# Two blocks of the last conditioning product moved from the router's stage into the wait of the linear attention, and one expert load held back for a gather

## The chip, the cores and the metric

The kernel runs on one core of one Trainium2 chip. The metric is the device time of one execution in microseconds (us). Three timed runs of the kernel before gave a median of 1047.66 us (1046.27 to 1048.70).

## The reference

Two layers of a diffusion backbone over 256 latent tokens `x` and 256 context tokens `ctx`, width 1024, all float32. Cut to what the change touches:

```python
for l in range(DEPTH):                                   # DEPTH = 2
    mod = (silu_c @ ada_w[l] + ada_b[l])                 # shift, scale, gate twice: 6 x 1024
    cmod = silu_cc @ ada_w[l] + ada_b[l]
    h_lat, h_ctx = modulate(x, sh1, sc1), modulate(ctx, csh1, csc1)
    if l % 2 == 0:                                       # layer 0
        o_ctx, s_f, s_b = even_mixer(h_ctx, 0, 0, ...)   # linear attention | convolution, one output projection
        o_lat, _, _ = even_mixer(h_lat, s_f, s_b, ...)
    else:                                                # layer 1: attention
        o_lat, o_ctx = odd_mixer(...)
    x = x + g1 * o_lat
    y = hier_moe(tokens, ...)                            # top-1 group of 4, top-2 experts of 4 in it
    x = x + g2 * y
return rms_norm(x) * final_norm_g

# gla_chunked, per head (4 heads), chunks of 64 tokens, in both directions:
att = where(mask, q_t @ k_t.T, 0)                        # scores inside a chunk
u   = k_end.T @ v                                        # what a chunk adds to the state
s   = decay * s + u                                      # recurrence over the chunks
o   = att @ v + q_t @ s_prev                             # inside + across
```

## The kernel before

Everything is written out by hand for the five engines, which meet only at semaphores. TensorE (PE) runs, in this order: the input projections of layer 0, `gla`, `even_out`, `rows_and_router(0)`, `experts(0)`, the attention of layer 1, its output projection, `rows_and_router(1)` and `experts(1)`. Products write one of eight PSUM banks `ps[:, b, :]` of 512 columns.

**Weights** go through a ring of six slots of 2 MB (`ring`, three more blocks have places of their own in `xh` and `gm`). `weight_stream` lists the blocks in the order in which PE uses them, and `ring_places` gives each block the slot of the block that is freed six before it. SyncE (SP) issues the loads in that order (`load`, L515; in the expert loop L563) and waits before each until PE has freed its slot, so a load can't be issued before the block six places ahead of it has been used. Behind the input projections the list was `eout` 0 and 1 (the two halves of the output projection), `ada` 8 to 11 of layer 1, then the experts: `g`, `u`, `d` for gate, up and down of one expert. `moe_stream` issues for layer 0: g0, u0, g1, u1, d0, g2, then u2, whose place in `xh` is free once the router's rows have been read (`h2_ps`), then d1 and so on.

**Conditioning.** `ada_block(g, n)` (L627) multiplies the two conditioning vectors by a 2 MB block of `ada_w`, 16 matmuls of 512 columns. Group 4 is the last third of layer 1's: its four blocks all add into bank 5 (`ADA_BANK[4]`). VectorE's (DVE) `ada_added(4)` (L1829) adds that bank to the bias row once all four are done, and PE waits for this before the first expert's down product. Two of the blocks ran in the router's first wait (while DVE chose the experts, `chosen`), two behind the index products of the first two experts.

**Linear attention** (`gla`) treats the four heads as two pairs `pt`. For each pair PE turns the decayed keys (`turn_keys`, L847), makes the scores, which DVE masks and adds (`masked`, L2398 and L2406) into SBUF, makes the chunk sums u for the directions d = 0, 1 (`chunk_sums`), the part inside the chunks (`inside`, L874), and, once DVE's `recurrence` (L2418, L2421) has written 14 states, the part `across` (L888). ScalarE (ACT) copies the turned keys (`keys_taken`, L1641), copies and squares the outputs (`outputs_taken`, L1648), and takes roots (`output_roots`, L1657) of what `square_sums` adds up on PE. `KV_BANK` names the banks of the chunk sums, `O_BANK` those of the outputs. The sum of squares of a head was written over its own output's bank. `even_out` (L948) starts with the convolution's channels (c = 4 to 7) and comes to the attention's channels when DVE has normed them (`normed_outputs`).

**Router and first gather.** In `rows_and_router(0)` PE turns the normed rows back (L975), ACT stores them to `h2_rows` in DRAM, DVE picks the experts and the row numbers. GpSimd (POOL) then gathers the first expert's 96 rows from DRAM (L2654, semaphore `xg_in0`), PE makes the slot product (L614, `ps<-ar` 128x32, waits `slots_ready`), turns the gathered rows (`first_xt`, L1136) and starts the experts' gate and up products (L614 and L1054).

## Time and profile before

| | us |
|---|---|
| median of three timed runs | 1047.66 |
| the profiled execution, its own time | 1039.51 |
| its span in the trace | 1037.7 |
| PE busy | 949.4 (91% of the span) |
| DVE busy | 623.6 (60%) |
| ACT busy | 178.0 (17%) |
| POOL busy | 114.9 (11%) |
| moved by DMA | 311.94 MB, mean 301 GB/s |

Busy shares are means over stages with different limits. Linear attention lies at 219 to 256 us of the span, the output projection at 256 to 316, the router at 316 to 352, the experts of layer 0 at 352 to 616, the attention of layer 1 to about 790, the experts of layer 1 from about 812. "PEclk" is the clock that TensorE was granted, in parts of 2.4 GHz: 0.50 is 1.2 GHz. A float32 matmul counts as two records. "Idle before <-releaser" is the time an engine stood before an instruction, and what ended it.

### The profile page before, as it was taken

Reading aid. Unit: us, or ns where it says so; the run is one execution under the profiler, and the core shown is the slowest. Engines: PE = TensorE matmul, PEld = TensorE weight load, DVE = VectorE, ACT = ScalarE, POOL = GpSimd, SP = SyncE. Lnnn points to the kernel's source line nnn. Section 1 sums busy time; section 2 is a strip of 40 time slices with the busy share of each in tenths; the row PEclk is TensorE's granted clock in tenths of the full one; section 3 lists DMA queues with packets and bytes.
Section 4 is the critical chain, followed back from the end, with each engine's and each line's share of the span. In section 5 each row is a group of like instructions: output and inputs, shape, how many; then the busy total and the mean of one; then the engine's idle time right before and its main releaser. Section 6 shows DMA issues by size and latency. Waiting matters only on the chain.

```text
span 1037.7 us, 19786 instructions
## 1 busy us (share of the span) xinstructions
PE 949.4 (91%) x7940; PEld 575.5 (55%) x7940; DVE 623.6 (60%) x1516; ACT 178.0 (17%) x339; POOL 114.9 (11%) x176
## 2 busy tenths in 40 slices
PE   3999999989998799999999997997997999988896
PEld 1443433457445588988988973443646455543442
DVE  1200799787456586676675636467435977775553
ACT  2100022353024010000000013225413000000001
POOL 7100100102300100000001132100101100000000
PEclk9999999997999699999999998999997999999999
DMA  9999876442826999999999959646034989999994
GB/s 332 398 392 369 327 268 218 164 163 84 250 91 243 383 357 362 403 417 405 391 402 407 424 181 356 245 167 237 6 104 180 346 339 400 399 385 412 417 429 171
DMA packets 51354, 311.94 MB, mean 301 GB/s; under 512 B 7096, under 2 KB 8888, under 8 KB 33632
## 3 DMA queue, kind: packets, MB, share of 16 engines
q1 hardware_dynamic: 36752, 277.88, 68.2%
q0 software_dynamic: 9376, 21.19, 6.7%
q10 hardware_dynamic: 5168, 12.06, 3.1%
q8 instruction: 41, 0.67, 0.3%
q14 instruction: 17, 0.14, 0.0%
HBM read 300.52 MB, written 17.25 MB: 306 GB/s over the span
## 4 chain that ended last, share of the span: by engine, by line
PE 69%; DMA 16%; DVE 9%; issue 2%; SPq 2%; ACT 2%; POOL 0%; ACTq 0%; DVEq 0%; POOLq 0%
PE ps L614 46%; PE ps L1054 9%; DMA ring<-in_moe_w_gate 8%; PE ps L948 3%; PE ps L627 3%; DMA ring<-in_moe_w_down 2%; DMA ring<-in_ada_w 2%; PE ps L1097 2%; PE ps L1175 2%; SPq L515 2%; DMA y_rows<-ar 1%; PE ps L888 1%; DMA xh<-y_rows,sm 1%; DMA ar<-h_rows,sm 1%; PE ps L1418 1%
## 5 line engine op out<-in xcount | busy, mean ns | idle before, releaser
L614 PE MATMUL ps<-ring,ar 128*32 128x384 f32 (+6 forms) x3872 | 479.8, 466 | 17.9 <-DMA ring<-in_moe_w_gate 13.7
L614 PEld LDWEIGHTS ps<-ring,ar 128*32 128x32 f32 (+2 forms) x3872 | 198.7, 121 | 145.3 <-issue 87.1
L1054 PE MATMUL ps<-ring,ar 128*32 128x128 f32 x1488 | 167.8, 275 | 0.0
L1054 PEld LDWEIGHTS ps<-ring,ar 128*32 128x32 f32 x1488 | 163.7, 111 | 2.7
L2171 DVE STREAM_TRANSPOSE ar<-ar 32x256 f32<-32x256 f32 x304 | 132.2, 435 | 5.0 <-issue 0.6
L614 PE MATMUL ps<-xh,ring 128*128 128x512 f32 x256 | 114.9, 603 | 0.7 <-DMA ring<-in_even_w_in 0.7
L2214 DVE TENSOR_TENSOR ar<-ar,ps 128x384 f32<-128x384 f32 (+2 forms) x33 | 15.9, 482 | 132.1 <-PE ps L1054 68.1
L614 PE MATMUL ps<-ring,xh 128*128 128x512 f32 x192 | 85.9, 604 | 1.9 <-ACT xh L1478 1.6
L614 PEld LDWEIGHTS ps<-xh,ring 128*128 128x128 f32 x256 | 48.3, 192 | 64.2 <-issue 62.9
L2343 DVE SCALAR_TENSOR_TENSOR ar<-ar,cpar 128x512 f32<-128x512 f32 x120 | 79.6, 742 | 0.0
L1530 ACT ACTIVATE ar<-ps 128x384 f32<-128x384 f32 (+2 forms) x33 | 14.3, 433 | 289.7 <-PE ps L614 205.7
L614 PEld LDWEIGHTS ps<-ring,xh 128*128 128x128 f32 x192 | 36.5, 193 | 48.6 <-issue 45.6
L2201 DVE STREAM_TRANSPOSE ar<-ar 32x64 f32<-32x64 f32 x256 | 60.5, 236 | 4.5
L2193 DVE STREAM_TRANSPOSE ar<-ar 32x128 f32<-32x128 f32 x144 | 59.5, 413 | 2.9
L1097 PE MATMUL ps<-ring,ar 128*32 128x256 f32 x256 | 57.9, 379 | 0.0
L2650 POOL COPY sm<-sm 96x1 int32 (+3 forms) x32 | 6.0, 187 | 342.4 <-DVE ar L2171 318.3
L627 PE MATMUL ps<-ring,silu_c 128*32 128x512 f32 x320 | 39.9, 619 | 0.0
L2311 DVE TENSOR_TENSOR ar<-ps,gm 128x512 f32<-128x512 f32 x12 | 8.3, 689 | 51.7 <-PE ps L614 39.8
L1097 PEld LDWEIGHTS ps<-ring,ar 128*32 128x32 f32 x256 | 28.0, 110 | 18.1
L614 PE MATMUL ps<-ar 128*128 128x512 f32 (+3 forms) x112 | 33.3, 464 | 4.6 <-ACT ar L1767 2.4
L1535 ACT ACTIVATE ar<-ps 128x512 f32<-128x512 f32 x16 | 9.6, 598 | 149.3 <-PE ps L614 149.3
L2654 POOL DMA_INDIRECT ar<-h_rows,sm x32 | 31.2, 976 | 27.9 <-POOL sm L2650 26.8
(371 smaller groups left out, 908.9 us busy)
## 6 DMA issues: line engine op xcount, KB each, us to landing
ring<-in_moe_w_gate SPq DMA_DIRECT2D x31, 2048.0 KB, 17.1
ring<-in_moe_w_up SPq DMA_DIRECT2D x30, 2048.0 KB, 15.6
ring<-in_moe_w_down SPq DMA_DIRECT2D x30, 2048.0 KB, 19.1
ring<-in_ada_w SPq DMA_DIRECT2D x24, 2048.0 KB, 10.5
ring<-in_even_w_in SPq DMA_DIRECT2D x5, 2048.0 KB, 14.0
y_rows<-ar POOLq DMA_DIRECT2D x17, 384.0 KB, 10.5
ring<-in_odd_w_in SPq DMA_DIRECT2D x3, 2048.0 KB, 18.1
y_rows<-ar ACTq DMA_DIRECT2D x16, 288.0 KB, 8.9
```

The source lines that it names most:

```text
L515: sp.dma_start(wide, s).then_inc(arrival(i), 16)
L614: return nc.tensor.matmul(o, l, r, start=start, stop=stop)
L627: m = nc.tensor.matmul(ps[32 * q:32 * q + 32, ADA_BANK[g], :], silu_c[:, 2 * k + c, 10 - 2 * s:42 - 2 * s], w[:, c, 512 * q:512 * q + 512] ...
L948: m = nc.tensor.matmul(ps[:, j, :], mix[:, c, j * P:(j + 1) * P], blk(i)[:, c, :], start=(c == 4), stop=(c == 3), skip_group_check=True)
L1054: m = nc.tensor.matmul(ps[96:128, bank, g * P:(g + 1) * P], xgT[:, p, c, 32 * g:32 * g + 32], w[:, c, 3 * P:HID], start=c == 0 and g == 0, ...
L1097: nc.tensor.matmul(ps[96:128, 5, 256 * g:256 * g + 256], tokens(g, c), w[:, c, 768:D], start=c == 0 and g == 0, stop=c == HC - 1 and g == ...
L1175: m = nc.tensor.matmul(acc(j, h), mixw[64 * h:64 * h + 64, p, j * P:(j + 1) * P], yb[64 * h:64 * h + 64, p, 0:512], start=False, stop=True ...
L2171: m = V.transpose(xgT[32 * q:32 * q + 32, p, :, slots], xg[slots, p, :].rearrange("s (c q i) -> s q c i", c=KC, q=4)[:, q, :, :])
L2193: V.transpose(hidT[32 * q:32 * q + 32, p, :, 32 * r:32 * r + 32], cols[:, q, :, :])
L2201: m = V.transpose(hidT[32 * q:32 * q + 32, p, 0:2, 32 * r:32 * r + 32], cols[:, q, :, :])
L2343: V.scalar_tensor_tensor(acc[n], u_in[:, n, :, bass.ds(t, 256)], cpar[:, n, bass.ds(t, 1)], acc[n], ALU.mult, ALU.add).then_inc(sem("conv_ ...
L2654: G.indirect_dma_start(xg[0:CAP[l], p, :], None, h2_rows, bass.IndirectOffsetOnAxis(ap=idxc[0:CAP[l], p:p + 1], axis=0), bounds_check=NT * ...
```

## The change

1. Blocks 8 and 9 of layer 1's `ada` stand in the stream ahead of `eout`. PE runs them (group 4, n = 0 and 1) in `gla` ahead of `across(0)`, into bank 6; DVE adds them between `decayed(1)` and `masked(1)`, and `scores(1)` waits for that, since it writes bank 6.
2. Blocks 10 and 11 (n = 2, 3) take the place of 8 and 9 in the router's first wait, into bank 5. Nothing stands any more behind the index products. DVE's `late_added` stands where `ada_added(4)` stood.
3. `chunk_sums(0, 1)` is cut in two: the even chunks (bank 1) go ahead of `inside(0, 0)`, the odd ones stay. `chunk_sums(1, 1)` writes banks 0 and 2 in place of 5 and 7 and moves ahead of `inside(1, 0)`, behind a wait for the first two outputs' copies.
4. The sums of squares have banks of their own (`SQ_BANK`); those of heads 0 and 1 move behind `inside(1, 1)`, and `even_out` no longer waits for the first two roots. ACT takes the second pair's keys before the first pair's outputs.
5. SP waits for the first gather's landing before it issues u2 of layer 0.

```diff
-    tail = [("eout", 0, 0), ("eout", 0, 1)] + ada(1, 8, 9, 10, 11) + moe_blocks(0)
+    tail = ada(1, 8, 9) + [("eout", 0, 0), ("eout", 0, 1)] + ada(1, 10, 11) + moe_blocks(0)
...
-        KV_BANK = (((4, 5), (1, 3)), ((1, 3), (5, 7)))
+        KV_BANK, SQ_BANK = (((4, 5), (1, 3)), ((1, 3), (0, 2))), ((5, 7), (4, 6))
...
-        ADA_BANK = (6, 2, 3, 2, 5)
+        ADA_BANK = (6, 2, 3, 2, 6)
+        LATE_BANK = 5
...
                     sp.wait_ge(sem("h2_ps"), NT)
+                    sp.wait_ge(sem("xg_in0"), 16)
                     expert_load("u", 2)
...
-                            m = nc.tensor.matmul(ps[32 * q:32 * q + 32, ADA_BANK[g], :],
+                            m = nc.tensor.matmul(ps[32 * q:32 * q + 32, LATE_BANK if g == 4 and n >= 2 else ADA_BANK[g], :],
...
-                chunk_sums(0, 0)
+                chunk_sums(0, 0).then_inc(sem("kv_sum"), 1)
                 pe.wait_ge(sem("att_masked"), 2)
+                chunk_sums(0, 1, range(0, NCH, 2))
                 inside(0, 0)
                 pe.wait_ge(sem("att_masked"), 4)
-                chunk_sums(0, 1)
+                chunk_sums(0, 1, range(1, NCH, 2)).then_inc(sem("kv_sum"), 1)
                 inside(0, 1)
                 pe.wait_ge(sem("qk_exp"), 8)
                 pe.wait_ge(sem("ke_diff"), 4)
+                ada_block(4, 0)
+                ada_block(4, 1)
                 across(0)
                 turn_keys(1)
+                pe.wait_ge(sem("ada_added"), 6)
                 scores(1)
-                square_sums((0, 1))
                 pe.wait_ge(sem("ketok_ready"), 4)
-                chunk_sums(1, 0)
+                chunk_sums(1, 0).then_inc(sem("kv_sum"), 1)
+                pe.wait_ge(sem("o_taken"), 2)
+                chunk_sums(1, 1).then_inc(sem("kv_sum"), 1)
                 pe.wait_ge(sem("att_masked"), 6)
                 inside(1, 0)
                 pe.wait_ge(sem("att_masked"), 8)
-                chunk_sums(1, 1)
                 inside(1, 1)
+                square_sums((0, 1))
                 across(1)
...
                 pe.wait_ge(sem("conv_ready"), NPT)
-                pe.wait_ge(sem("o_root"), 2)
...
                 if l == 0:
                     pe.wait_ge(sem("h2_act"), 2)
-                    ada_block(4, 0)
-                    ada_block(4, 1)
+                    ada_block(4, 2)
+                    ada_block(4, 3)
...
-                    pe.wait_ge(sem("h2_act"), NT)
-                    ada_block(4, 2)
-                    ada_block(4, 3)
...
+                keys_taken(1)
                 outputs_taken(0)
-                keys_taken(1)
...
                 decayed(1)
+                ada_added(4)
                 masked(1)
```

PE's program from the turned keys of the second pair to the end of linear attention; `ar,xh 64x128` are chunk sums, L874 (now L877) is `inside`, `ar,cst 128x512` the sums of squares, L888 (now L891) `across`. Before:

```order
L614 MATMUL ps<-xh 128x128 x15
L614 MATMUL ps<-ar,cst 128x512 [waits o_taken] x2
L614 MATMUL ps<-ar,xh 64x128 [waits ketok_ready]
L614 MATMUL ps<-ar,xh 64x128 x15
L874 MATMUL ps<-xh,ar 128x128 [waits att_masked]
L874 MATMUL ps<-xh,ar 128x128 x3
L614 MATMUL ps<-ar,xh 64x128 [waits att_masked]
L614 MATMUL ps<-ar,xh 64x128 x15
L874 MATMUL ps<-xh,ar 128x128 x4
L888 MATMUL ps<-xh,ar 128x64 [waits state]
```

The same place in the changed kernel:

```order
L616 MATMUL ps<-xh 128x128 x15
L616 MATMUL ps<-ar,xh 64x128 [waits ketok_ready]
L616 MATMUL ps<-ar,xh 64x128 x15
L616 MATMUL ps<-ar,xh 64x128 [waits o_taken]
L616 MATMUL ps<-ar,xh 64x128 x15
L877 MATMUL ps<-xh,ar 128x128 [waits att_masked]
L877 MATMUL ps<-xh,ar 128x128 x3
L877 MATMUL ps<-xh,ar 128x128 [waits att_masked]
L877 MATMUL ps<-xh,ar 128x128 x3
L616 MATMUL ps<-ar,cst 128x512 [waits o_taken] x2
L891 MATMUL ps<-xh,ar 128x64 [waits state]
```

Both directions' chunk sums now stand ahead of the first wait for the masks, and the sums of squares behind both `inside`. SP's loads around the router in the changed kernel (`ring` is a ring slot, `xh` the place of u2):

```order
L516 DMA ring<-in_moe_w_down 128x4096 [waits block_used]
L516 DMA ring<-in_moe_w_gate 128x4096 [waits block_used]
L516 DMA xh<-in_moe_w_up 128x4096 [waits xg_in0,h2_ps]
L516 DMA ring<-in_moe_w_down 128x4096 [waits block_used]
L516 DMA ring<-in_moe_w_gate 128x4096 [waits block_used]
```

These are d0, g2, u2, d1 and g3. The order of the expert loads is the old one; what each waits for has moved: g0 and u0 now wait for `ada` 8 and 9, g1 and u1 for `eout` 0 and 1, d0 and g2 for `ada` 10 and 11.

## Rows read from the trace of the kernel before

**Rows 1.** Page, the chain that ended last, shares by engine
```profile
PE 69%; DMA 16%; DVE 9%; issue 2%; SPq 2%; ACT 2%; POOL 0%; ACTq 0%; DVEq 0%; POOLq 0%
```

**Rows 2.** Timeline, PE, linear attention: start, us, what, [idle before <-releaser]
```profile
219.36 1.04 PE L847 MATMUL ps<-cst,gm 128*128 128x128 f32 x8
220.32 2.06 PE L614 MATMUL ps<-gm 64*128 64x128 f32 x32
...
227.09 1.16 PE L874 MATMUL ps<-gm,ar 128*128 128x128 f32 x8
230.84 6.03 PE L888 MATMUL ps<-gm,ar 64*128 64x64 f32 x56 [2.59 <-DVE ar L2421]
236.80 1.97 PE L847 MATMUL ps<-cst,xh 128*128 128x128 f32 x8
238.69 3.30 PE L614 MATMUL ps<-xh 64*128 64x128 f32 x32
...
250.57 5.36 PE L888 MATMUL ps<-xh,ar 64*128 64x64 f32 x56 [2.42 <-DVE ar L2421]
255.86 4.95 PE L948 MATMUL ps<-ring,ar 128*128 128x512 f32 x8
...
262.36 24.20 PE L948 MATMUL ps<-ring,ar 128*128 128x512 f32 x56
```

**Rows 3.** Windows: stretch, length, busy PE PEld DVE ACT POOL, PEclk, DMA share, GB/s
```profile
228.00:231.00 3.00, 0.41 (x6) 0.25 (x5) 3.00 (x12) 2.99 (x4) 0.00 (x0) 1.00 0.00 0
231.00:233.00 2.00, 2.00 (x23) 2.00 (x23) 2.00 (x4) 2.00 (x4) 0.00 (x0) 0.52 0.00 0
...
253.00:256.00 3.00, 3.00 (x29) 2.88 (x27) 2.93 (x4) 0.05 (x1) 0.00 (x0) 0.50 0.00 0
```

**Rows 4.** Timeline, DVE, linear attention
```profile
227.51 3.17 DVE L2421 SCALAR_TENSOR_TENSOR ar<-ar,ps 128x128 f32<-128x128 f32 x12
...
238.09 0.48 DVE L2390 MEMSET xh<- 128x512 f32 x1 [3.79 <-PE ps L847]
...
247.13 0.29 DVE L2418 COPY ar<-ps 128x128 f32<-128x128 f32 x1 [1.33 <-PE ps L614]
```

**Rows 5.** Timeline, ACT, the second pair's keys
```profile
239.29 1.08 ACT L1641 ACTIVATE xh<-ps 128x512 f32<-128x512 f32 x2
```

**Rows 6.** Timeline, SP, the four `ada` loads and g0
```profile
180.98 38.94 SPq L515 DMA_DIRECT2D ring<-in_ada_w  x4
286.59 0.34 SPq L515 DMA_DIRECT2D ring<-in_moe_w_gate  x1
```

**Rows 7.** Timeline, PE, router to the first expert
```profile
327.70 3.64 PE L627 MATMUL ps<-ring,silu_c 128*32 128x512 f32 x32
...
341.63 1.97 PE L614 MATMUL ps<-ar 128*128 128x32 f32 x16 [0.57 <-DVE ar L2060]
349.66 1.51 PE L1136 MATMUL ps<-cst,ar 96*128 96x96 f32 x8 [6.06 <-DMA ar<-h_rows,sm]
351.96 0.86 PE L614 MATMUL ps<-ring,ar 128*32 128x384 f32 x3 [0.78 <-DVE ar L2165]
```

**Rows 8.** Gathers of `h2_rows`: first of layer 0, four in its experts, first of layer 1
```profile
L2654 POOL DMA_INDIRECT ar<-h_rows,sm x1: 1025/1025/1025, 339.1 to 339.1; - x1
DMA to landing us min/median/max: 10.4/10.4/10.4
...
DMA to landing us min/median/max: 9.5/10.2/10.8
...
DMA to landing us min/median/max: 3.0/3.0/3.0
```

**Rows 9.** Windows, first experts, columns as in rows 3
```profile
356.00:364.00 8.00, 8.00 (x141) 7.80 (x133) 6.20 (x16) 0.49 (x1) 0.51 (x2) 0.91 1.01 367
```

**Rows 10.** Expert loads issued 400 to 530 us, and PE's waits at 480 to 600
```profile
DMA to landing us min/median/max: 9.7/18.2/28.6
...
PE ps L614 <- DMA ring<-in_moe_w_gate: 2.0, 2, 1.9
```

More of the change, by code:

```diff
@@ L463, in ada_last @@
             l, a, n = ADA_GROUPS[g]
-            return at["ada", l, 2 + h if g == 0 else 2 * (a + n) - 1]
+            return at["ada", l, 2 + h if g == 0 else 9 if g == 4 else 2 * (a + n) - 1]
         def xn_of(k):
@@ L626, in ada_block @@
                         for q in range(4):
-                            m = nc.tensor.matmul(ps[32 * q:32 * q + 32, ADA_BANK[g], :],
+                            m = nc.tensor.matmul(ps[32 * q:32 * q + 32, LATE_BANK if g == 4 and n >= 2 else ADA_BANK[g], :],
                                                  silu_c[:, 2 * k + c, 10 - 2 * s:42 - 2 * s], w[:, c, 512 * q:512 * q + 512],
-                                                 start=n == 0 and c == 0, stop=True, skip_group_check=True)
+                                                 start=n == (2 if g == 4 and n >= 2 else 0) and c == 0, stop=True,
+                                                 skip_group_check=True)
                     m.then_inc(sem("block_used"), 1)
@@ L837, in square_sums @@
                     pe.wait_ge(sem("o_taken"), h + 1)
-                    mm(ps[:, O_BANK[h // 2][h % 2], :], ones, (qT if h % 2 == 0 else kT)[:, h // 2, :])\
+                    mm(ps[:, SQ_BANK[h // 2][h % 2], :], ones, (qT if h % 2 == 0 else kT)[:, h // 2, :])\
                         .then_inc(sem("o_sumsq"), 1)
@@ L860, in scores, with chunk_sums @@
                         m.then_inc(sem("att"), 1)
-                def chunk_sums(pt, d):
-                    for n in range(NCH):
+                def chunk_sums(pt, d, chunks=range(NCH)):
+                    for n in chunks:
                         lo = CHUNK * (n % 2)
@@ L869, in chunk_sums @@
                                    v_tok[lo:lo + 64, n // 2, (2 * pt + hh) * P:(2 * pt + hh + 1) * P])
-                    m.then_inc(sem("kv_sum"), 1)
+                    return m
                 def inside(pt, hh):
@@ L1159, in down @@
                 if l == 0 and isinstance(e, int) and e == 0:
-                    pe.wait_ge(sem("ada_added"), 6)
+                    pe.wait_ge(sem("ada_added"), 7)
                 if not (isinstance(e, int) and e == 0) and not narrow(l, e):
@@ L1656, in output_roots @@
                     act.wait_ge(sem("o_sumsq"), 2 * pt + hh + 1)
-                    A_((qT if hh == 0 else kT)[:, pt, :], ps[:, O_BANK[pt][hh], :], ACT.Sqrt, scale=1.0 / DV, bias=eps)\
+                    A_((qT if hh == 0 else kT)[:, pt, :], ps[:, SQ_BANK[pt][hh], :], ACT.Sqrt, scale=1.0 / DV, bias=eps)\
                         .then_inc(sem("o_root"), 1)
@@ L1830, in ada_added, with late_added @@
                                            ALU.add, ALU.add).then_inc(sem("ada_added"), 1)
+            def late_added():
+                dve.wait_ge(sem("block_used"), at["ada", 1, 11] + 1)
+                V.tensor_tensor(modrow_of(4), modrow_of(4), ps[:, LATE_BANK, :], ALU.add).then_inc(sem("ada_added"), 1)
             def mean_square(n, width, count):
@@ L2243, in experts @@
                     rows_placed()
-                    ada_added(4)
+                    late_added()
                 if l == 1:
@@ L2596, in mod_rows @@
                 l, a, n = ADA_GROUPS[g]
-                pool.wait_ge(sem("ada_added"), g + 2)
+                pool.wait_ge(sem("ada_added"), 7 if g == 4 else g + 2)
                 for s in range(n // 2):
```

## The prediction, made before the changed kernel was run

> **What bounds the kernel now.** I read the chain that ended last first. It is 69% PE, 16% DMA and 9% DVE [rows 1], so PE's own order decides most of the time, and what can be gained lies in the places where PE stands or is slow. Next, PE's timeline with its idle times. Linear attention has two: 2.59 us before `across(0)` and 2.42 us before `across(1)`, both ended by DVE's recurrence [rows 2]. The windows beside them show what follows: PE was busy for 0.41 of the 3 us before 231, and from 231 on the granted clock was 0.52, that is 1.2 GHz; the second idle ends in 0.50 at 253 to 256 [rows 3]. So `turn_keys(1)` took 1.97 us where the same eight records had taken 1.04, and `scores(1)` 3.30 where they had taken 2.06 [rows 2]. In the router PE stood 6.06 us for the first expert's gather, which took 10.4 us from issue to landing [rows 7, 8], and ran the first experts at the low clock. After that PE has work without a break until late in the loop, where it waits 1.9 us for a gate load [rows 10]. What is won before 352 us therefore moves the whole rest, unless the loads don't follow.
>
> **Linear attention.** (a) The even half of `chunk_sums(0, 1)`, 0.55 us, goes into PE's wait for the second mask, so `inside(0, 1)`, which ended at 228.25 (227.09 + 1.16), ends at about 227.7. The two blocks cost what two cost in the router, 3.64 us at the full clock [rows 7], and end at 231.35. The states were there for 230.84 [rows 2]: `across(0)` starts at 231.4, **0.6 us late**. (b) PE now has no gap of any size between 220 and 231, and I take the clock to stay full. `across(0)` isn't in the trace at full clock; the eight turned keys give a ratio of 1.97 to 1.04, so 6.03 becomes 3.2. That is 2.8, with 0.9 for the keys and 1.2 for the scores **4.9 us**. `scores(1)` ended at 242.0 and now ends at 237.7. (c) From there DVE leads: masks, sums, recurrence. In it DVE stood 1.33 us for `chunk_sums(1, 1)`, which waited for the last mask itself [rows 4]. It now runs ahead of `inside(1, 0)`: **1.3 us**. Its new wait is for ACT: two copies of keys in 1.08 us [rows 5], then four copies and squares of a bank, which I put at the same length or a little more each, begun half a microsecond behind `across(0)` at 235.2 and done at about 238.9, while PE reaches the wait at 238.8. Behind it stand `inside(1, 0)` and `inside(1, 1)` and the sums of squares, two matmuls of 512 columns each like those of the projection (0.43 a record, 24.20 / 56 [rows 2]), some 5 us in all but for the wait for the last mask, done by about 244.6, and the recurrence, 3.6 us behind the last mask at 241.2, ends at 244.8. So `across(1)` starts at 244.9 where it started at 250.57, with almost no idle before it. (d) Then it too runs at the full clock, 3.2 for 5.36: **2.1 us**. The first eight records of `even_out` took 4.95 where 56 took 24.20, so 3.5 at full clock: **1.4 us**. The sum is 4.9 - 0.6 + 1.3 + 2.1 + 1.4 = **9.1 us** by the first sums of `even_out`.
>
> What I cost at nothing here: DVE's added `ada_added(4)` (0.7 us) lies in the 3.79 us in which DVE stood for the turned keys [rows 4]; without this cover it would delay the masks by its length. The dropped wait for two roots ended long before PE came to it, and the other banks change no time by themselves. The first root comes at about 244.3, just ahead of DVE's norming at 244.8; a late one has some 10 us of cover, as DVE norms a pair of heads in about 10 us and `even_out` first does 12 us of convolution channels and then 3.4 us for each attention channel. The loads of `eout` move from the first to the second places and `ada` 8 and 9 forward; the four places of `ada` were at 181 to 220 [rows 6], so `eout` is issued some 60 us before its use, and `ada` 8 and 9 before 181. g0 is issued at about 230 in place of 286.6 [rows 6], u0 behind it; they share the DMA engines with POOL's gate rows, which are first needed when `even_out` has its first half. Without that cover the gate rows would be late by the gather's difference under load, some 7 us [rows 8].
>
> **Router.** Its chain of DVE steps is untouched, so everything is 9.1 us earlier. The gather was issued at 339.14 and is now issued at about 330.0. In the trace u1 was still under way then, and d0, g2 and u2 were issued within 3 us of it. Now g1 and u1 landed long ago; only d0 and g2 are in flight. They wait for the two blocks in the router's first wait, which ran at 327.7 to 331.3 [rows 7] and now run 9.1 earlier, so they are issued at 320.5 and 322.3. Two loads of 2 MB and the last rows stored are some 5.5 MB, at about 400 GB/s 13.5 us: through at about 334.5. A gather takes 3.0 us with no load beside it and 9.5 to 10.8 with loads [rows 8]. Of its work 4.5/10.4 is done by 334.5 and the rest goes at the free rate: 334.5 + 0.57 x 3.0 = 336.2. The bounds are 333.0 (free throughout) and 340.4 (loaded throughout). PE's slot product is now a rival for the same place. It waits for DVE until 341.6 - 9.1 = 332.5, but PE has stood since the index products ended at about 326.6, where two blocks used to run, so I expect 1.2 GHz: 1.97 [rows 7], by the ratio of the turned keys, becomes 3.7, and it ends at 336.2 too. `first_xt` starts at 336.3. Of the 349.66 it had, 9.1 was counted; the rest is **4.3 us**.
>
> **Clock in the first experts.** The low clock lay over `first_xt` and over the first experts up to 357.4: 8 us at 0.91 [rows 9] are 1.4 us at 0.50 behind 356. The experts began at 351.96 [rows 7], so 5.4 us at half speed, 2.7 us lost. Ahead of them PE had stood 6 us; now it has the slot product there and goes on into `first_xt`. The clock should be full sooner after the experts' start; the bounds are 0 (as late as before) and 2.7 (full at once). I take a little over half, **1.5 us**, because this stretch is nearer to the linear attention, where the low clock ended while PE went on without a gap, than to a stretch that follows an idle of 6 us.
>
> **The expert loop.** SP now holds u2 until the gather has landed, at about 336. Behind it in SP's order stands d1, which can't go before g0 has been used at about 345, so nothing queued behind the wait is late; u2 itself, 8 to 13 us to landing, is needed some 37 us behind the start. The loop loads keep their distance to PE: the lag from issue to landing was back at 9.7 us at 400 and grew to 28.6 at 530 [rows 10], so a lead won before 352 is gone by 400, and the 2 us of waits near the end stay. `late_added` costs what `ada_added(4)` cost. The rest moves as it stands.
>
> **Sum.** 9.1 + 4.3 + 1.5 = **14.9 us**. The profiled execution took 1039.51 us (span 1037.7), so it would take 1024.6. It was 8.2 us or 0.8% below the median of the timed runs; the terms are idle times and PE's cycles, which I don't scale. Median: 1047.66 - 14.9 = **1032.8 us**.
>
> **The rivals.**
> A. *The gather is no faster.* It lands 10.4 us behind its issue whatever is queued, at 340.4: the four gathers among the experts took 9.5 to 10.8 [rows 8] while the loads' lag varied. What remains is 9.1 and 0.1: 9.2 us, 1038.5. For it: d0 and g2 may last longer than 334.5. Against it: 3.0 us where none ran. The Trainium skill, page "DMA: Bandwidth & Descriptors", section "Queues, rings and completion order", has each DMA engine take turns between the queue rows that have work, a packet at a time. By this rule it matters only whether a load is queued, not how many, and holding u2 back brings nothing by itself; the trace agrees (10.4 with several queued, 9.5 at the least in the loop), and what speeds the gather is that d0 and g2 run out under it.
> B. *The clock falls in spite of the two blocks.* Then `across(0)` starts 0.6 late and stays slow with all behind it: 1.3 - 0.6 + 4.3 + 1.5 = 6.5 us, 1041.2. For it: the blocks were never seen ahead of `across`; against: with them in the router's first wait the clock stayed at full, and the low clock came only behind gaps.
> C. *The router's clock holds.* The slot product takes 1.97 us, the gather ends the wait at 336.2 or sooner, `first_xt` (1.51) and the first expert run at full clock: 14.9 + 0.7 + 1.2 + up to 1, some 17.5 us, 1030.2. Against it: PE stands longer there than ever before.
> D. *A and B together*: 0.7 + 0.1, no change that can be told, 1046.9.
> E. *Slower: the loads fall behind in the loop of layer 0.* 41 loads are issued there behind u2. The lag grew by 18.9 us over 26 of them to 28.6, where PE began to wait [rows 10]. From there each further microsecond of load time is one of PE's. If a load took 0.4 us longer than now, 41 of them would cost 16 us and eat the gain; at 0.5 us it is 1053. For it: no slack is left at 530. Against it: neither the loads, their order nor what shares the engines in the loop is changed.
>
> **How the numbers follow.** Forecast 60%, A 16%, B 10%, C 8%, D 3%, E 3%. About 0.2% (2.1 us) is what a measurement of this kernel can tell from no change. Faster: forecast, A, B and C, 0.94; same: D, 0.03; slower: E, 0.03. The bounds of the forecast's own terms (the clock term 0 to 2.7, the slot product 1.97 to 3.7, the gather 333.0 to 340.4) and the runs' spread of 1.2 us make it 1029.5 to 1036. The range takes in C and A and leaves out B, D and E: 1029.5 to 1040.
>
> **What would show each step.** Two conditioning blocks at about 227.7 to 231.4 with the clock at 1.00 through 256; `across(0)` and `across(1)` at about 3.2 us each; no wait of DVE before its second state copy; the second pair's chunk sums waiting under 0.3 us for ACT; the first sums of `even_out` at about 247 to 248. In the router a gather of some 6 us, the slot product at 3.7 us and low clock, `first_xt` near 336.3, full clock some 2 us behind the first expert's start. In the loop loads with a lag that grows to some 28 us, and about 2 us of PE's waits. The prediction is wrong if the clock falls at 231 all the same, if the gather takes 10 us, or if PE waits for loads by more than a few microseconds.

## The result, and the profile after

| | median us | lowest to highest | runs |
|---|---|---|---|
| before, beside the change | 1048.18 | 1046.27 to 1049.07 | 4 |
| changed | 1032.88 | 1030.84 to 1037.06 | 4 |
| profiled execution of before | 1039.51 | span 1037.7 | |
| profiled execution of the change | 1033.16 | span 1031.3 | |

The ratio is 0.9877, with a 95% interval of 0.9844 to 0.9910. The forecast was 1032.8 us in a range of 1029.5 to 1040: the number is right. Two further comparisons of the same kernel gave 0.9856 (0.9811 to 0.9900) and 0.9856 (0.9821 to 0.9892), at 1032.96 and 1032.17 us. The two profiled executions lie only 6.4 us apart, though (the forecast had the profiled one at 1024.6 us, and it took 1033.16), and how the 15 us come about is not quite what the forecast said. Two slow executions of the kernel before, of 1259.6 and 5198.7 us, are counted in no ratio and no range here.

The executions also begin differently. The first turned keys of linear attention, which nothing of the change precedes on PE, start at 219.36 us in the profile before and at 221.49 in that of the change. I therefore count from that row, called **T0** below, in every profile: "T0 + 34.4" is 34.4 us behind the start of that row.

PE's timeline in linear attention, the changed kernel; it answers to [rows 2] (start, us, what, [idle before <-releaser]):

```profile
221.49 1.04 PE L850 MATMUL ps<-cst,gm 128*128 128x128 f32 x8
...
226.08 1.09 PE L616 MATMUL ps<-ar,gm 64*64 64x128 f32 x16 [0.54 <-DVE gm L2414]
...
228.19 1.09 PE L616 MATMUL ps<-ar,gm 64*64 64x128 f32 x16
229.21 1.16 PE L877 MATMUL ps<-gm,ar 128*128 128x128 f32 x8
230.30 3.64 PE L629 MATMUL ps<-ring,silu_c 128*32 128x512 f32 x32
233.87 3.34 PE L891 MATMUL ps<-gm,ar 64*128 64x64 f32 x56
237.14 1.09 PE L850 MATMUL ps<-cst,xh 128*128 128x128 f32 x8
238.16 2.06 PE L616 MATMUL ps<-xh 64*128 64x128 f32 x32
...
247.38 3.34 PE L891 MATMUL ps<-xh,ar 64*128 64x64 f32 x56 [0.62 <-DVE ar L2429]
250.66 3.70 PE L955 MATMUL ps<-ring,ar 128*128 128x512 f32 x8
...
255.91 24.20 PE L955 MATMUL ps<-ring,ar 128*128 128x512 f32 x56
```

The two blocks stand in the gap, and everything behind them runs at full clock: `across(0)` 3.34 for 6.03 us, the keys 1.09 for 1.97, the scores 2.06 for 3.30, `across(1)` 3.34 for 5.36. One thing is not as drawn up: each half of `chunk_sums(0, 1)` took 1.09 us, where the whole had taken 1.10. The first 56 records of `even_out` behind the sums of squares start at 255.91, that is T0 + 34.4 where they started at T0 + 43.0. **Linear attention gave 8.6 us.**

PE in the router, the same profile, for [rows 7]:

```profile
335.19 3.62 PE L616 MATMUL ps<-ar 128*128 128x32 f32 x16 [4.65 <-DVE ar L2068]
340.57 1.51 PE L1140 MATMUL ps<-cst,ar 96*128 96x96 f32 x8 [1.76 <-DMA ar<-h_rows,sm]
342.90 0.86 PE L616 MATMUL ps<-ring,ar 128*32 128x384 f32 x3 [0.81 <-DVE ar L2173]
```

Its windows (the columns are those of [rows 3]), and the gather of h rows from issue to landing, for [rows 8]:

```profile
327.00:330.00 3.00, 2.17 (x14) 2.17 (x14) 2.81 (x10) 0.00 (x0) 0.00 (x0) 0.61 1.02 437
...
336.00:339.00 3.00, 2.81 (x14) 2.68 (x13) 0.08 (x1) 0.00 (x0) 0.00 (x1) 0.50 0.80 195
...
345.00:348.00 3.00, 3.00 (x34) 2.64 (x30) 2.58 (x14) 0.00 (x0) 0.00 (x0) 0.50 0.87 358
```

```profile
DMA to landing us min/median/max: 7.7/7.7/7.7
```

PE's wait for the gather fell from 6.06 to 1.76 us, since the gather now lands 7.7 us behind its issue and the slot product fills most of that time. It does so at the low clock (3.62 us), which lasts to 348.2, 5.3 us into the first expert, as long as in the profile of before (5.4). The experts start at T0 + 121.4, before at T0 + 132.6: **11.2 us by here**.

From here on the forecast let everything move as it stands. It does not. At the end of layer 0, where the last expert is narrow, PE has six gaps and then a fallen clock (PE's timeline, then a window that holds the last of them, the changed kernel):

```profile
598.38 0.44 PE L616 MATMUL ps<-ring,ar 128*32 128x128 f32 x6 [0.33 <-issue]
...
601.37 0.37 PE L616 MATMUL ps<-ring,ar 128*32 128x128 f32 x1 [0.17 <-issue]
602.08 3.35 PE L616 MATMUL ps<-ring,ar 128*32 128x128 f32 x63 [0.34 <-issue]
```

```profile
600.00:606.00 6.00, 5.18 (x88) 3.69 (x90) 0.82 (x3) 0.28 (x1) 1.98 (x3) 0.72 0.83 316
```

Neither is in the profile of before, whose row of these narrow products and the first wide one behind it are:

```profile
604.60 5.61 PE L614 MATMUL ps<-ring,ar 128*32 128x256 f32 x160
...
610.03 0.61 PE L614 MATMUL ps<-ring,ar 128*32 128x512 f32 x3
```

The narrow products took 5.4 us before (604.60 to 610.03) and take 10.7 now (594.36 to the first wide one at 605.08). The six gaps themselves are only 1.8 us of that: between them PE got through 1 to 6 records in 0.73 us, where it had done 160 in 5.61. From the start of the experts to the mixing of their last rows it took 264.9 us before (616.87 - 351.96) and takes 270.6 now (613.46 - 342.90).

### The profile page after: what moved, and what is told of

It is laid out like the page before. It is cut to its first block, busy times and chain, and to the rows that moved or that the text cites. A ratio compares the mean times of both kernels' runs of the same rounds, so it can differ in the third digit from the quotient of the medians.

```text
span 1031.3 us, 19788 instructions
## 1 busy us (share of the span) xinstructions
PE 952.6 (92%) x7940; PEld 574.0 (56%) x7940; DVE 623.7 (60%) x1517; ACT 177.6 (17%) x339; POOL 114.7 (11%) x176
## 4 chain that ended last, share of the span: by engine, by line
PE 73%; DMA 13%; DVE 8%; issue 2%; SPq 2%; ACT 2%; ACTq 0%; POOL 0%; DVEq 0%; POOLq 0%
PE ps L616 48%; DMA ring<-in_moe_w_gate 10%; PE ps L1058 10%; PE ps L629 3%; PE ps L955 3%; PE ps L1101 2%; DMA ring<-in_ada_w 2%; PE ps L1179 2%; SPq L516 2%; PE ps L1422 1%; DMA ar<-h_rows,sm 1%; PE ps L891 1%; DVE ss L2540 1%; DVE xh L1870 1%; PE ps L1214 0%
## 5 line engine op out<-in xcount | busy, mean ns | idle before, releaser
L616 PE MATMUL ps<-ring,ar 128*32 128x384 f32 (+6 forms) x3872 | 485.3, 469 | 17.5 <-DMA ring<-in_moe_w_gate 11.2
L1534 ACT ACTIVATE ar<-ps 128x384 f32<-128x384 f32 (+2 forms) x33 | 14.3, 432 | 291.8 <-PE ps L616 203.8
## 6 DMA issues: line engine op xcount, KB each, us to landing
y_rows<-ar POOLq DMA_DIRECT2D x17, 384.0 KB, 10.7
```

The source lines that it names most:

```text
L616: return nc.tensor.matmul(o, l, r, start=start, stop=stop)
```

## The experiments

Each time is the median, and each ratio is to the kernel before, run beside the variants on the same chip. There were three groups of variants. In the first (the change again, without the hold, each part alone) the kernel before was at 1047.2 us (19 runs, 1041.2 to 1052.0), in the second (the kernel before again, the two filled kernels, the later gathers) at 1040.4, in the third (the last four below) at 1046.4; the second and the third ran on the same chip.

**The change again.** Edit: none.

> The changed kernel again, nothing edited. In its first profile PE was 10.2 us ahead of the kernel before at 606 and only 3.4 us ahead at the end of the last expert of layer 0: its matmuls between 598 and 612 stood in gaps of 0.3 us put down to issue, and the granted clock fell to 0.59 at 600 to 604. If that belongs to the one execution, a second profile has no such gaps, the last expert ends some 10 us ahead and the profiled execution takes about 1027 to 1030. If it comes with the change (POOL's gathers of y rows start 10 us earlier, before the last loads), the gaps are there again and it takes about 1033. Timed against the kernel before: 14 to 15.5 us faster.

1032.96 us, ratio 0.9856. The profiled execution took 1031.41. At the end of layer 0 it has the same six gaps of 0.3 us, from 597.48 to 601.13. PE's timeline there, the narrow products up to the first gap and then the first wide one:

```profile
593.00 4.18 PE L616 MATMUL ps<-ring,ar 128*32 128x256 f32 x98
...
602.52 0.62 PE L616 MATMUL ps<-ring,ar 128*32 128x512 f32 x3
```

So the gaps are not an accident of one execution; the forecast of 1027 to 1030 without them fell. The fallen clock at 600 was one: here it stayed full until 615, and the narrow products took 9.5 us, 4.1 more than in the kernel before, by the gaps and the slow progress between them alone. Up to the experts the profile agrees with the first within 0.1 us (T0 + 34.4, T0 + 121.5).

**Without the hold.**

```diff
-                    sp.wait_ge(sem("xg_in0"), 16)
```

> SP no longer holds the third up load for the gather. If fewer loads beside the gather are what made it land 7.75 us behind its issue and not 10.4, it goes back to about 10 us, PE waits for it until some 343 in place of 340.5 and the time is 2 to 2.5 us above the changed kernel. If it matters only whether any load is queued (the rival A of the prediction), the gather takes 7.7 us again and the time is the same within 0.7 us.

1036.68 us, 3.7 above the change. PE's timeline in the router of this kernel:

```profile
334.09 3.62 PE L615 MATMUL ps<-ar 128*128 128x32 f32 x16 [5.84 <-DVE ar L2067]
342.44 1.51 PE L1139 MATMUL ps<-cst,ar 96*128 96x96 f32 x8 [4.73 <-DMA ar<-h_rows,sm]
```

The gather takes 10.7 us with one more load of 2 MB in front of it, and 7.7 with that load held. Rival A is out: what is queued beside the gather counts, and in the changed kernel the hold is worth about 3 us at `first_xt` and 3.7 in the time. The hold in the kernel before, without the rest of the change, was not run.

**The new order alone.** The four blocks, the ring's order and the banks of the conditioning sums as before, and no hold; of linear attention's order this is left:

```diff
-                ada_block(4, 0)
-                ada_block(4, 1)
                 across(0)
                 turn_keys(1)
-                pe.wait_ge(sem("ada_added"), 6)
                 scores(1)
```

> The new order of linear attention alone: the four conditioning blocks back in the router, the places of the ring as before, no hold. If the two blocks are what holds the clock, it falls at about 231 as in the kernel before, across(0) takes 6.0, the keys 1.97, the scores 3.3 us, DVE's state copies come without the 1.33 us wait, and the time is 1 to 2.5 us under the kernel before. If the order holds the clock itself, across(0) takes 3.3 us and the time is 7 to 9 us under it. I expect the first.

**The two blocks alone.** The order, the banks of states and sums of squares and ACT's order as before, no hold:

```diff
                 pe.wait_ge(sem("ke_diff"), 4)
+                ada_block(4, 0)
+                ada_block(4, 1)
                 across(0)
                 turn_keys(1)
+                pe.wait_ge(sem("ada_added"), 6)
                 scores(1)
                 square_sums((0, 1))
```

> The two conditioning blocks in linear attention alone, with the order of before around them and no hold. If they hold the clock, across(0) takes 3.3, the keys 1.1 and the scores 2.06 us (5.0 us won, less the 0.9 by which the blocks start it late), DVE still waits 1.3 us before its second state copy, and PE's wait before across(1) is still there at 2 us or more; whether the clock survives that wait is open: with it across(1) and the first sums of even_out give 3.3 us more. In the router the slot product takes 3.6 us at the low clock and the gather about 10. In sum 5 to 10 us under the kernel before; if the blocks did nothing for the clock, 0 to 1 us above it.

1042.57 and 1042.21 us (10 runs each, 1034.9 to 1046.5 and 1038.4 to 1043.7), 4.7 and 5.0 under the kernel before. The 95% intervals of the ratios are 0.9909 to 0.9980 and 0.9924 to 0.9978, so each of the two gains may be anything from 2 us to 8 (the blocks) or 9.5 (the order). PE's timeline, first of the new order alone, then of the blocks alone:

```profile
231.59 4.92 PE L889 MATMUL ps<-gm,ar 64*128 64x64 f32 x56 [2.59 <-DVE ar L2423]
...
238.34 2.78 PE L614 MATMUL ps<-xh 64*128 64x128 f32 x32
...
248.29 3.34 PE L889 MATMUL ps<-xh,ar 64*128 64x64 f32 x56 [0.62 <-DVE ar L2423]
251.56 3.70 PE L950 MATMUL ps<-ring,ar 128*128 128x512 f32 x8
```

```profile
232.45 3.34 PE L890 MATMUL ps<-gm,ar 64*128 64x64 f32 x56
...
236.74 2.06 PE L615 MATMUL ps<-xh 64*128 64x128 f32 x32
...
247.38 5.67 PE L890 MATMUL ps<-xh,ar 64*128 64x64 f32 x56 [2.42 <-DVE ar L2427]
252.97 6.32 PE L953 MATMUL ps<-ring,ar 128*128 128x512 f32 x8
```

Each part holds the clock at its own place. With the order alone it falls behind the gap of 2.59 us and is slow in `across(0)`; at `across(1)` the gap is 0.62 and the clock full. With the blocks alone it is the other way round, and the 2.42 us before `across(1)` cost 2.3 us there and 2.6 in the first sums of `even_out`. By the start of the 56 records of `even_out` (256.81 and 260.85, T0 at 220.12 and 220.06) the order alone is at T0 + 36.7, 6.3 us ahead of before, and the blocks alone at T0 + 40.8, 2.2 us ahead; together they are 8.6 ahead. I had looked for 1 to 2.5 us from the order alone and was wrong: I had not counted that it also closes the second gap. The two parts by themselves (4.7 and 5.0 us) and what the whole loses without the hold (3.7) add up to 13.4 of the 14.3 us that the whole gained in this group.

The profiles of the two parts do not show a gain at the end, though. From T0 to the end they take 817.5 and 818.2 us, the kernel before 818.3. Both have the six gaps of layer 0, and from the start of the experts to the mixing they take 273.4 and 268.5 us (617.80 - 344.44 and 619.23 - 350.75) where it took 264.9. What each part brings by the output projection is shown; what it is worth in the time rests on the medians alone.

**The kernel before again.** Edit: none.

> The kernel before again, nothing edited. Its first profile has no gaps put down to issue in the last experts of layer 0 and its time, 1039.5 us, is 8 us below its median; the profiles of the changed kernel (twice) and of the three part changes all have six or seven such gaps of 0.3 us at the narrow expert, with a fallen clock behind them. If these gaps are the normal case of this program, a second profile of the kernel before shows them too, the stretch from 600 to the mixing of the last expert's rows takes some 5 to 7 us longer than in the first profile, and the time is 1045 to 1049. If they come with the change, the second profile is like the first, at about 1040.

1041.36 us, against 1040.38: the same kernel, and both 5 to 8 us below what it took in the other groups and beside the change. In this profile PE has no gaps at the end of layer 0 either, and the stretch from the experts' start to the mixing takes 266.0 us (615.27 - 349.24). So no profile shows the gaps as a normal thing in the kernel before; they are in all three profiles of the changed kernel, in those of the parts, in those of the unsplit and the two fitted kernels below, and in neither of this one. What does differ is the router:

```profile
334.93 2.72 PE L614 MATMUL ps<-cst,ar 128*96 128x1 f32 x16 [1.48 <-DVE ar L2010]
337.58 5.69 PE L627 MATMUL ps<-ring,silu_c 128*32 128x512 f32 x32
343.20 1.97 PE L614 MATMUL ps<-ar 128*128 128x32 f32 x16
347.51 0.85 PE L1136 MATMUL ps<-cst,ar 96*128 96x96 f32 x8 [2.34 <-DMA ar<-h_rows,sm]
```

Here the clock fell one wait earlier, ahead of the index products, the two blocks ran slowly and ended late, and d0, which needs the place of one, went out at 341.28, behind the gather (339.80) and not ahead of it as in [rows 7, 8]'s profile. The gather took 7.6 us in place of 10.4, and the experts start at T0 + 129.3 in place of T0 + 132.6. The low clock lasted 2.8 us into them, not 5.4. SP's loads (queue q1: packets, MB, share of 16 engines) did not stop for this gather, as its stretch of 339.8 to 347.4 shows; q0 is the gather:

```profile
q1 hardware_dynamic: 168, 2.49, 85.5%
q0 software_dynamic: 122, 0.39, 14.9%
```

So a gather beside loads need not take 10 us: issued 0.9 us behind a load it took 10.4, issued 1.5 us ahead of that load 7.6, and in the profile of the new order alone, again 1.5 us ahead of it, 8.5. By its own spread the kernel before differs by 3 us at this place. Its own times lie between 1035 and 1052 us over all groups, those of the changed kernel between 1029.7 and 1037.1.

**PE kept busy in the router.** 154 records (77 products, two records each) that nobody reads:

```diff
+                    pe.wait_ge(sem("h2_act"), NT)
+                    for _ in range(10):
+                        mm(ps[:, 7, 0:P], ones, cst[:, C_TRI:C_TRI + P])
...
+                    for _ in range(45):
+                        mm(ps[:, 7, 0:P], ones, cst[:, C_TRI:C_TRI + P])
...
+                    for _ in range(22):
+                        mm(ps[:, 7, 0:P], ones, cst[:, C_TRI:C_TRI + P])
```

> The changed kernel with 77 products of 128 columns into an unused bank in PE's waits of the router: 10 before the index products, 45 behind them, 22 behind the slot product. They compute nothing that is read. If the low clock in the router comes from PE's waits alone, it stays full, the slot product takes 1.97 in place of 3.6 us and ends earlier, and the first experts run at full clock: first_xt 0.7 and the first expert 2.6 us shorter, 3 to 3.5 us under the changed kernel. The gather's landing does not change. If the clock falls all the same, the fillers take twice their time and the slot product starts some 4 us late: 2 to 5 us above the changed kernel.

**The same, and three loads held for the gather.**

```diff
-                expert_load("d", 0)
                 if l == 0:
-                    expert_load("g", 2)
                     sp.wait_ge(sem("h2_ps"), NT)
                     sp.wait_ge(sem("xg_in0"), 16)
+                expert_load("d", 0)
+                if l == 0:
+                    expert_load("g", 2)
                     expert_load("u", 2)
```

> As the filled kernel, and SP holds the first down load and the third gate load for the gather too, not the third up load alone. If it is the loads beside it that make the gather long, it now lands within 4 us of its issue, in time for the end of the slot product, and first_xt starts 3 us earlier than in the filled kernel. Whether that stays won: three loads come 10 us later, and if the loads have no slack before PE's first waits, it is given back there. I expect the filled kernel's time, within 2 us. If the gather's time did not depend on loads, it takes 7 to 8 us again and nothing moves at first_xt.

1033.40 and 1033.39 us, ratios 0.9920 and 0.9927 to a kernel before at 1040.4; no changed kernel ran beside them. The timeline of PE in the filled kernel, then its gather and that of the kernel with three loads held:

```profile
330.04 10.29 PE L616 MATMUL ps<-cst 128*128 128x128 f32 x90
340.17 1.87 PE L616 MATMUL ps<-ar 128*128 128x32 f32 x16
341.88 5.16 PE L616 MATMUL ps<-cst 128*128 128x128 f32 x44
```

```profile
DMA to landing us min/median/max: 5.7/6.3/6.9
```

```profile
DMA to landing us min/median/max: 4.0/4.3/4.7
```

The clock stays at 1.00 in every window from 321 to 357: it is PE's waits that lower it in the router. But one of these products is two records of 0.115 us, not one: the 45 take 10.3 us and not the 5 I had meant, so `first_xt` comes 6 us late and the gain is spent. The first expert's gather needs 6.9 us in the one and 4.0 in the other (issued at 332.88; SP, which waits for it, goes on at 336.96), for 7.7 in the changed kernel. PE did not need it so soon here, so this run says nothing on the hold's worth.

**The early gathers of y rows later.**

```diff
                 pool.wait_ge(sem("positions"), 1)
+                pool.wait_ge(sem("block_used"), at["u", 0, LAST] + 1)
                 for p in range(2):
```

> The changed kernel, with POOL's first gathers of stored y rows held until PE is through the last expert's up product. If these gathers, which run at 596 to 601 beside the narrow gate product, are what makes PE's gaps of 0.3 us and the fallen clock there, the gaps are gone and the last expert ends some 4 to 6 us earlier; the end of layer 0 then depends on how late the gathers are, between 5 us faster and 3 us slower in all. If the gaps have another cause, they stay at the same products and the time is the same or up to 5 us longer.

1033.74 us, ratio 0.9929, beside a kernel before at 1040.4. PE's timeline at the narrow expert, and its first row behind the mixing of layer 0:

```profile
595.95 5.61 PE L616 MATMUL ps<-ring,ar 128*32 128x256 f32 x159
```

```profile
622.79 1.97 PE L697 MATMUL ps<-cst,ar 128*128 128x128 f32 x8 [6.52 <-DVE ar L1924]
627.95 8.73 PE L616 MATMUL ps<-ring,xh 128*128 128x512 f32 x16 [3.19 <-DMA ring<-in_odd_w_in]
```

The gaps are gone, and the stretch from the experts to the mixing takes 265.1 us (608.19 - 343.06) in place of 270.6: without the gathers beside them there are no gaps. The time is not better all the same. PE now waits 6.5 us for the chain of gathers and sums behind the mixing, then 3.2 for a load.

**The even half not split off.**

```diff
                 pe.wait_ge(sem("att_masked"), 2)
-                chunk_sums(0, 1, range(0, NCH, 2))
                 inside(0, 0)
                 pe.wait_ge(sem("att_masked"), 4)
-                chunk_sums(0, 1, range(1, NCH, 2)).then_inc(sem("kv_sum"), 1)
+                chunk_sums(0, 1).then_inc(sem("kv_sum"), 1)
```

> The changed kernel with the other direction's chunk sums in one piece behind the second mask, as before. The whole took 1.10 us before and each half 1.09 in the changed kernel. If the split brings nothing because the halves cost as much as the whole, across(0) starts at the same distance from the first turned keys as in the changed kernel, 12.4 us, and the time is the same. If the split wins its 0.55 us, across(0) starts 0.5 us later here.

1033.05 us (3 runs), beside 1032.17 of the change. `across(0)` starts at 232.44 - 220.04 = T0 + 12.4, as in the changed kernel. The whole took 1.10 us again, behind a wait of 0.95 for the mask. The split brings nothing.

**The change once more.** Edit: none.

> The changed kernel, nothing edited, beside the three others of this call. 1031 to 1035 us. The kernel before was at 1047 us in one call and at 1040 to 1041 in another (itself and its copy), while kernels built on the changed one were at 1033 to 1034 in both. If the gain depends on which of its own times the kernel before shows, the ratio here lies anywhere from 0.986 to 0.993; if the first ratio was the rule, at 0.987.

1032.17 us, ratio 0.9856. In this profile the clock fell once in linear attention, behind the gap of 0.62 us that is left before `across(1)`: that took 3.81 us, and eight sums of `even_out` 4.86 for 3.70. It is the only one of the ten profiles with the new order and one or both of the blocks in which it did.

**One block ahead, and fillers that fit.** Block 8 alone before `across(0)`, 9 and 10 in the router's first wait, 11 behind the index products (the ring's order likewise), and the filler products 5, 16 and 14 in place of 10, 45 and 22:

```diff
-    tail = ada(1, 8, 9) + [("eout", 0, 0), ("eout", 0, 1)] + ada(1, 10, 11) + moe_blocks(0)
+    tail = ada(1, 8) + [("eout", 0, 0), ("eout", 0, 1)] + ada(1, 9, 10, 11) + moe_blocks(0)
...
                 ada_block(4, 0)
-                ada_block(4, 1)
                 across(0)
```

> One conditioning block ahead of across(0) and not two, two in the router's first wait, one behind the index products; and unread products there sized by what one took in the filled kernel, 0.23 us: 5 before the index products, 16 behind them, 14 behind the slot product. If the clock holds in both places, across(0) waits for the states and starts 0.9 us earlier than with two blocks, the slot product takes 1.9 us, first_xt starts where the gather lands, at the same distance as in the changed kernel, the first expert runs at full clock and starts 0.7 us sooner behind it, and the time is 3 to 4.5 us under the changed kernel if the loads follow, 0 to 2 if they take it back. If a wait of 0.9 us behind one block drops the clock, across(0) takes 5 to 6 us again and the gain is gone.

**The same with three loads held**, and no fillers behind the slot product.

> As the one before, with the first down load and the third gate load held for the gather too and no products behind the slot product. With all three loads held the gather landed 4.1 us behind its issue in place of 7.8. So first_xt starts where the slot product ends, some 3.3 us earlier than with one load held. Three loads come 10 us later than now: if there is slack, the time is 3 us under the kernel with one load held; if PE then waits for the loads in the loop, it is the same or up to 2 us above it.

1035.70 us with one load held, 3.5 above the change beside it, and 1033.48 with three, 1.3 above it. In the first, PE at `first_xt`, and SP's third gate load:

```profile
342.51 0.85 PE L1147 MATMUL ps<-cst,ar 96*128 96x96 f32 x8 [3.10 <-DMA ar<-h_rows,sm]
```

```profile
330.33 0.33 SPq L516 DMA_DIRECT2D ring<-in_moe_w_gate  x1
```

The block put behind the index products frees its place late, so the third gate load went out at 330.3, 1.4 us ahead of the gather, and the gather took 10.6 us again. Linear attention was 1.0 us shorter (254.97 - 221.55 = 33.4 for 34.4), as expected, but `first_xt` came at T0 + 121.0 where the changed kernel has it at T0 + 119.1.

The fillers kept the slot product at full clock, but behind them PE waited 3.1 us for the gather, and the first expert then ran for 3.4 us at the low clock (344.3 to 347.7).

With three loads held the lead is real at the start. PE at `first_xt` and at the first expert, and PE's waits for loads from 345 to 600:

```profile
335.81 1.51 PE L1146 MATMUL ps<-cst,ar 96*128 96x96 f32 x8 [0.71 <-DMA ar<-h_rows,sm]
338.10 0.86 PE L617 MATMUL ps<-ring,ar 128*32 128x384 f32 x3 [0.78 <-DVE ar L2179]
```

```profile
PE ps L617 <- DMA ring<-in_moe_w_gate: 5.9, 4, 2.4
```

The experts start at T0 + 117.7, 3.8 us ahead of the changed kernel, though the clock fell at `first_xt` behind a wait of only 0.71 us. In the loop PE then waits 5.9 us for gate loads where the changed kernel's three profiles have 1.5 to 2.0 (the kernel before has 2.0 in one profile and 4.2 in the other), and the mixing starts at 614.00, T0 + 393.6, behind the change's T0 + 392.0. The loads take back all of it.

## Why the prediction was right, and where it was not

The median, the range and the sign came out, the median in part by luck, as the last step shows. By its own steps:

- **Clock in linear attention: right**, and the largest part. Full clock from T0 on, `across` at 3.34 where 3.2 was estimated, no idle of DVE before the second state copies, 0.62 us left before `across(1)`. Forecast 9.1 us, measured 8.6.
- **The split of `chunk_sums(0, 1)`: wrong.** "The even half, 0.55 us, goes into PE's wait." A half costs 1.09 us, as much as the whole, so `across(0)` started 0.9 us late and not 0.6.
- **The slot product: right.** 3.7 us forecast at the low clock, 3.62 measured, and it is no longer what ends the wait.
- **The gather: right in its cause, too short.** Forecast 6.2 us from issue to landing, measured 7.7; without the hold 10.7. The loads ran out as worked out (counted from T0, at 334.5 + 2.1 = 336.6). The 195 GB/s at 336 to 339 are the gathers themselves, by the queues of this stretch (q0 the gathers, q1 SP's loads):

```profile
q0 software_dynamic: 174, 0.57, 76.4%
q1 hardware_dynamic: 2, 0.02, 3.6%
```

  What was wrong is the "free rate" of 3.0 us. It is that of layer 1's first gather, for which POOL writes 64 row numbers; for this one it writes 96, and with all three loads held it needed 4.0 and 4.2 us. Here the second expert's gather, issued 2.1 us behind it, also ran beside it. Nor was 4.5/10.4 of the work done when the loads ended: of the 0.7 MB of the two gathers, most moved behind 336. And the sentence that holding u2 back "brings nothing by itself" did not hold in this kernel: with d0 and g2 issued as early as now but u2 behind them, the gather took 10.7 us. `first_xt` starts at T0 + 119.1, 11.2 us ahead and not 13.4.
- **The clock in the first experts: wrong.** I took 1.5 us of a possible 2.7. Between the first two profiles it was 0: the low clock lasted 5.4 us into the experts before and 5.3 now. The second and third profiles of the changed kernel have 4.6 each, and the second of the kernel before has 2.8, so no gain shows in any pair, and the length varies by itself by 2.6 us. With fillers and no wait but one of 0.8 us the clock did not fall.
- **"The rest moves as it stands": wrong.** Of 11.2 us the mixing of layer 0 kept 5.5 (T0 + 397.5 before, T0 + 392.0 now). The narrow products with the gaps beside the y gathers took 5.3 us of this difference (4.1 in the second profile). The mixing itself then took 11.4 us for 8.1, since the clock fell at 617.8, in the middle of it. Part of all this was no loss, since before PE had been waiting at the next step, which is this row of the kernel before, and then that of the changed kernel's second profile:

```profile
630.38 1.97 PE L694 MATMUL ps<-cst,ar 128*128 128x128 f32 x8 [5.43 <-DVE ar L1916]
```

```profile
621.95 1.97 PE L697 MATMUL ps<-cst,ar 128*128 128x128 f32 x8
```

  Counted from T0 that is 411.0 and 402.6: 8.4 us of the gain get through, and about as much, 8.5 and 8.1, is left at the ends of the two profiles (span less T0: 818.3 before, 809.8 and 810.2). Against the second profile of before, which has this row at T0 + 409.3, it is 6.7.
- **The loop's loads: right.** PE waits 1.5 to 2.0 us for a gate load, as in the first profile of before. The run with three loads held shows how near rival E was: 3.8 us more lead and it is given back whole.
- **The step from the profile to the median: not accounted for.** I took 14.9 us off both. From T0 to the end the profiles show less: 818.3 and 819.8 us before, 809.8, 810.2 and 813.8 after, 8.5 us between the first of each. The medians show 14 to 15 in three comparisons; where the kernel before ran at 1040.4 us, three variants of the change, at 1033.4 to 1033.7, gained 7. The kernel before varies by 17 us over all its runs, and both its profiles are from the faster half of them all. The mean granted clock of each run gives a hint. In the first group it was 0.958 to 0.968 for the kernel before, median 0.962, and 0.969 to 0.970 for the changed one; the first profile of before had 0.967. By an estimate, 0.005 less of it in 1040 us are 10.4 us more at half speed, worth 5.2 us. But the second profile of before, at 1041.6 us, had 0.961, so the clock alone does not order the runs. What the slower ones contain besides, perhaps gaps like those of the changed kernel, no profile here tells, and some 6 us of the measured difference stay open. So the forecast hit the median by luck: 3.7 us too much up to the experts (14.9 against 11.2) and 2.7 more lost at the end of layer 0 were made up by this part, of which it knew nothing. By the profiles alone the gain behind T0 was 8.5 us and not 14.9.

## What to carry to other kernels

A few microseconds of work from elsewhere, put into a wait, can be worth more than their own length: here two blocks of 3.6 us cost 0.9 and kept the clock for the 10 us behind them. But every gap of that size needs its filler: each of the two, left open by itself, lowered the clock again behind it. And a lead on an engine counts only as far as the loads and the next chain follow: one variant that brought PE 3.8 us further ahead at the experts, and one that brought it 5.4 further ahead at the mixing, ended no sooner.

## What the runs showed of the hardware

- **Half of a group of matmuls that share a row half is no cheaper.** 32 records of 64*64 tiles, chunk by chunk on one half of the rows and then on the other, took 1.10 us; the 16 of the even chunks, all on one half, took 1.09, the 16 odd ones 1.09. That fits an overlap of neighbours on different halves, which sorting them by half takes away; I measured no other split.
- **The length of a gather of 96 rows follows the loads that are queued ahead of it**: 10.7 us with u2 queued, 10.6 with g2 issued 1.4 us ahead of it, 6.9 to 7.9 with both of d0 and g2 running out under it, 4.0 to 4.2 with all three held. With the next load issued 1.5 us behind it, it took 7.6 and 8.5, though loads moved beside it all the time. Rival A's conclusion, that it matters only whether a load is queued, does not hold by that. The Trainium skill, "DMA: Bandwidth & Descriptors", section "Queues, rings and completion order", has each DMA engine take turns between the queue rows it has work for. The traces do not contradict this, but no run tells it from another way of sharing.
- **PE stood in gaps of 0.3 us, six times 0.73 us apart, at the narrow products**, in each of the nine profiles in which they appeared 2.0 to 2.1 us behind POOL's first gather of y rows (595.45 and 597.48; 596.28 and 598.38). They and the slow progress between them made 5.4 us of products into 9.5. With the gathers held they were gone. In both profiles of before and of the filled kernels the gathers ran beside the same products without them, so the gathers are needed but not enough; what else it takes is open. The supply of instructions to PE is a candidate that no run here tests.
- **The same idle time does not always lower the clock at once**: behind the 0.62 us before `across(1)` it fell in one profile of eleven, behind 2.4 to 2.6 us in each of the four profiles that had such a gap. In the fitted kernel with three loads held it fell behind 0.71 us, and with one load held only some 2 us behind a wait of 3.1.
